# Attention values with the heads' values as 64-column weights and the probabilities moving

## What is computed

```python
# fox_prompt, one block of 128 queries
s = einsum('bqhd,bshd->bhqs', qi, kp) * SCALE + c_q - c_k      # masked to kpos <= qpos
p = softmax(s)
out = einsum('bhqs,bshd->bqhd', p, vp)
# swa: p = exp(s + bias - m) / (sum(exp(s + bias - m)) + exp(sink - m)), out = p @ v
fo = fox(...) * silu(fg); so = swa(...) * silu(sg)
y = layer_norm(ALPHA * x + concat([fo, so]) @ w_out)
```

## Time and profile before

| | us |
|---|---|
| median of 3 runs | 1110.37 |
| lowest, highest | 1108.74, 1110.75 |
| the profiled execution | 1110.16 |
| its span on the core | 1108.6 |
| TensorE busy | 1082.8 (98%) |
| VectorE busy | 556.2 (50%) |
| ScalarE busy | 470.8 (42%) |
| clock granted to TensorE, mean share of full speed | 0.995 |

### The profile page before, as it was taken

How to read it: one execution, slowest core, us unless ns; L and a number is a source line. 1 busy time by engine, 2 the same in 40 slices (tenths; PEclk the granted TensorE clock), 3 DMA queues, 4 the chain that set the end, 5 groups by cost and what they waited for, 6 DMA issues and landing times.

```text
span 1108.6 us, 21056 instructions
## 1 busy us (share of the span) xinstructions
PE 1082.8 (98%) x7697; PEld 1039.1 (94%) x7697; DVE 556.2 (50%) x1330; ACT 470.8 (42%) x1235; POOL 50.4 (5%) x99
## 2 busy tenths in 40 slices
PE   6999999999999999999999999999999999999996
PEld 6999999999999999999999999999999888888885
DVE  6654354444535444444543665453665474424486
ACT  5344444444444444444444555544555553112300
POOL 1010000000000000000000000000000000000000
PEclk9999999999999999999999999999999999999998
DMA  8132223212222222123522122122121216322423
GB/s 336 41 133 88 71 98 105 89 60 106 81 75 98 72 84 87 69 98 105 165 91 96 47 76 83 46 88 86 60 76 52 76 42 243 115 76 76 160 87 114
DMA packets 20376, 106.62 MB, mean 96 GB/s; under 512 B 3168, under 2 KB 3584, under 8 KB 11056
## 3 DMA queue, kind: packets, MB, share of 16 engines
q1 hardware_dynamic: 14528, 83.12, 21.1%
q0 software_dynamic: 5808, 22.95, 6.2%
HBM read 95.18 MB, written 14.17 MB: 99 GB/s over the span
## 4 chain that ended last, share of the span: by engine, by line
PE 97%; DVE 1%; issue 1%; ACT 0%; DMA 0%; DVEq 0%; SPq 0%; ACTq 0%
PE ps L1139 61%; PE ps L1288 19%; PE ps L1248 8%; PE ps L1230 4%; PE ps L1213 2%; PE ps L1214 2%; PE ps L1167 1%; PE ps L1260 1%; PE ps L1272 1%; DMA x_raw<-in_xT 0%; DVE rows L1108 0%; DVE rows L1118 0%; ACT k L640 0%; PE ps L1262 0%; DVE xl L939 0%
## 5 line engine op out<-in xcount | busy, mean ns | idle before, releaser
L1139 PE MATMUL ps<-xh,wh 128*128 128x288 f32 (+1 forms) x1664 | 508.4, 306 | 0.0
L1139 PE MATMUL ps<-xl,wh 128*128 128x288 f32 (+1 forms) x1664 | 492.9, 296 | 0.0
L1139 PE MATMUL ps<-xh,wl 128*128 128x288 f32 (+1 forms) x1664 | 492.4, 296 | 0.0
L1139 PEld LDWEIGHTS ps<-xh,wh 128*128 128x128 f32 x1664 | 313.7, 189 | 0.8 <-DVE wl L944 0.3
L1139 PEld LDWEIGHTS ps<-xl,wh 128*128 128x128 f32 x1664 | 314.1, 189 | 0.0
L1139 PEld LDWEIGHTS ps<-xh,wl 128*128 128x128 f32 x1664 | 313.2, 188 | 0.0
L798 DVE TENSOR_TENSOR wl<-w_raw,wh 128x1024 fp32r<-128x1024 f32 x132 | 159.8, 1218 | 74.5 <-ACT wh L611 72.5
L1288 PE MATMUL ps<-wh,mix_parts 128*128 128x512 f32 x576 | 186.9, 393 | 0.7 <-issue 0.7
L658 ACT ACTIVATE tb<-tb,small 128x256 f32<-128x256 f32 (+5 forms) x160 | 82.4, 515 | 214.1 <-DVE small L886 145.3
L611 ACT ACTIVATE wh<-w_raw 128x1024 fp32r<-128x1024 f32 x132 | 137.9, 1053 | 73.6 <-PE ps L1288 67.5
L1288 PEld LDWEIGHTS ps<-wh,mix_parts 128*128 128x128 f32 x576 | 108.9, 189 | 23.5 <-issue 0.9
(11 more groups left out here) (116 smaller groups left out, 888.3 us busy)
## 6 DMA issues: line engine op xcount, KB each, us to landing
w_raw<-in_w_all SPq DMA_DIRECT2D x66, 1024.0 KB, 4.8
cbc<-c_rows POOLq DMA_DIRECT2D x16, 360.0 KB, 4.2
x_raw<-in_xT SPq DMA_DIRECT2D x8, 592.0 KB, 10.0
rows<-in_x_p POOLq DMA_DIRECT2D x4, 1024.0 KB, 10.6
out_y_p<-rows SPq DMA_DIRECT2D x16, 256.0 KB, 2.5
rel_copies<-rel_rows POOLq DMA_DIRECT2D x1, 3072.0 KB, 16.2
out_fvT<-vT POOLq DMA_DIRECT2D x8, 296.0 KB, 2.4
out_fkT<-kT POOLq DMA_DIRECT2D x8, 296.0 KB, 2.4
```

What stands on the lines that cost most here:

```text
L1139: ins = nc.tensor.matmul(ps[:, st.bank(k, h), 0:width], a[k % 2][:, w], b[:, ko, first:first + width], start=(ko == 0 and i == 0), stop=(k ...
```

## The change

The division moves ahead of the product: after the reciprocal VectorE multiplies the unit's row of probabilities by it, in place (`tensor_scalar`, 160 of them, 144 to 528 columns), and `turn` waits for that (`scaled`) in place of the exponential (`exp_done`). `values` is called once for both heads of a query tile, at the second head's step: for each block and head the 64 columns of `v_nat` are the weights and `pt` moves, 128 columns wide (64 for the sample), and head 0 writes PSUM partitions 0 to 63, head 1 partitions 64 to 127 of the same bank. So the result lies as the gate wants it; `turn_heads`, `normalize` and `o_nat` are gone, and the gate reads the bank of the values. `pt` gets three slots in place of two. In the last stretch a unit is turned three steps after its score instead of two.

```diff
         if final:
-            score, turn, value = [[u + c for u in range(10)] for c in (1, 3, 5)]
+            score, turn, value = [[u + c for u in range(10)] for c in (1, 4, 5)]
...
-                if u >= 2:
-                    act.wait_ge(valued, 10 * st.g + u - 1)
+                if u >= 3:
+                    act.wait_ge(valued, 5 * st.g + (u - 3) // 2 + 1)
...
-            def normalize(st, u):
-
-                index, head = UNITS[u]
-                slot, n = u % 5, 10 * st.g + u + 1
-                act.wait_ge(valued, n)
-                act.wait_ge(recip_done, n)
-                nc.scalar.activation(o_nat[:, index, HD * head:HD * head + HD], ps[:, st.value_bank(u), 0:HD],
-                                     ACT.Copy, scale=recip[:, slot:slot + 1]).then_inc(value_read, 1)
...
                 nc.vector.reciprocal(rc, t).then_inc(recip_done, 1)
...
+                row = tb[:, u % SLOTS, 0:st.kind.keys(QTILE[UNITS[u][0]])]
+                dve.wait_ge(recip_done, n)
+                nc.vector.tensor_scalar(row, row, rc, None, ALU.mult).then_inc(scaled, 1)
...
-                pe.wait_ge(exp_done, 10 * st.g + u + 1)
+                pe.wait_ge(scaled, 10 * st.g + u + 1)
...
+                first, q = (P * tile, P) if tile < 4 else (0, DEC_SEQ)
                 for j, (_, w, block_) in enumerate(blocks):
-                    weights = pt[:, u % 2, j, :] if w == P else pt_meta[:, u % 2, :]
-                    ins = nc.tensor.matmul(ps[:, st.value_bank(u), 0:HD], weights,
-                                           v_nat[:, block_, HD * head:HD * head + HD],
-                                           start=(j == 0), stop=(j == len(blocks) - 1))
+                    for head in range(2):
+                        slot = (2 * index + head) % 3
+                        moving = pt[:, slot, j, 0:q] if w == P else pt_meta[:, slot, :]
+                        ins = nc.tensor.matmul(ps[head_rows(head), st.value_bank(tile), first:first + q],
+                                               v_nat[:, block_, HD * head:HD * head + HD], moving,
+                                               start=(j == 0), stop=(j == len(blocks) - 1))
                 ins.then_inc(valued, 1)
-
-            def turn_heads(st, g):
-
-                pe.wait_ge(value_read, 10 * g + 10)
-                if g is st.turn_before:
-                    pe.wait_ge(v_ready, 4 * st.kvs)
-                for index in (3, 2, 1, 0):
-                    tile = QTILE[index]
-                    ins = nc.tensor.transpose(ps[:, st.heads_bank(0), tile * P:(tile + 1) * P], o_nat[:, index, :], ident[:])
-                ins.then_inc(heads_turned, 1)
-                nc.tensor.transpose(ps[:, st.heads_bank(1), 0:P], o_nat[:, 4, :], ident[:]).then_inc(heads_turned, 1)
```

More of the change, by code:

```diff
@@ L236, in turn_bank, with value_bank_before, value_bank @@
         return 6 if self.final else 4 + p % 2
-    def value_bank(self, u):
-        return 7 if self.final else 6 + u % 2
-    def heads_bank(self, part):
-        return (6 if self.final else 4) + part
+    @staticmethod
+    def value_bank_before(tile):
+        return 6 if tile < 4 else 7
+    def value_bank(self, tile):
+        if self.final:
+            return 7 if tile < 4 else 5
+        return self.value_bank_before(tile)
 def build(nc, xT, w_all, w_ff, b_f, lf_cache, k_cache, v_cache, sinks, rel, keep_k, keep_v,
@@ L587, in _ @@
             whole(pool, run)
-            over = -(-4 * D_MODEL // TOK)
+            over = -(-4 * D_MODEL // NQ)
             for m in range(MT):
@@ L749, in run @@
                         keep_turned(st, u)
-                    for u in st.at(st.value_at, s - 1):
-                        normalize(st, u)
                     if st.kv is not None and s == CACHED_AT:
@@ L1232, in turn, with values @@
                     ins.then_inc(turned, 1)
-            def values(st, u):
-                index, head = UNITS[u]
+            def values(st, index):
                 tile = QTILE[index]
@@ L1239, in values @@
                 pieces = len(st.kind.blocks(tile))
-                if tile == 4 and head == 0:
+                if tile == 4:
                     pe.wait_ge(v_cached, 16 * st.kvs)
-                if u >= st.depth:
-                    pe.wait_ge(value_read, 10 * st.g + u - st.depth + 1)
-                pe.wait_ge(turned_read, st.kind.base(st.g) + st.kind.first(u) + pieces)
-                for j, (_, w, block_) in enumerate(blocks):
-                    weights = pt[:, u % 2, j, :] if w == P else pt_meta[:, u % 2, :]
-                    ins = nc.tensor.matmul(ps[:, st.value_bank(u), 0:HD], weights,
-                                           v_nat[:, block_, HD * head:HD * head + HD],
-                                           start=(j == 0), stop=(j == len(blocks) - 1))
@@ L1251, in values @@
[L1251 to L1262 removed]
+                    if st.final:
+                        pe.wait_ge(score_read, st.kind.base(st.g) + st.kind.PIECES)
@@ new lines, in values @@
+                if index == 0 and st.kind is Swa:
+                    pe.wait_ge(gated, 2 * st.g)
+                pe.wait_ge(turned_read, st.kind.base(st.g) + st.kind.first(2 * index + 1) + pieces)
+                first, q = (P * tile, P) if tile < 4 else (0, DEC_SEQ)
+                for j, (_, w, block_) in enumerate(blocks):
+                    for head in range(2):
[4 more added lines that the diff above has]
+                                               start=(j == 0), stop=(j == len(blocks) - 1))
@@ L1268, in turn_values @@
                 if st.kind:
+                    pe.wait_ge(turned_read, st.kind.base(st.g) + st.kind.PIECES)
                     pe.wait_ge(gated, 2 * st.g + (0 if st.keep else 2))
@@ L1322, in run @@
                     for u in st.at(st.value_at, s):
-                        values(st, u)
+                        if u % 2:
+                            values(st, u // 2)
                     for u in st.at(st.turn_at, s):
@@ L1327, in run @@
                         score(st, u)
-                    if st.turn_before is not None and s == st.before_at:
-                        turn_heads(st, st.turn_before)
-                    if s == st.out_at:
-                        turn_heads(st, st.g)
                     if s == st.v_at:
```

52 lines of the change are left out of this document (24 added, 28 removed).

## The result

The changed kernel takes **1112.73 us** in the median of seven runs (1111.28 to 1114.07), the kernel before beside it 1109.33 (1107.61 to 1110.75). The ratio is 1.0028, 95% interval 1.0019 to 1.0037: slower by 3 us, where 25 us less were forecast. Its profiled execution has a span of 1111.1 us, against 1108.6 before.

What follows compares the result with a forecast made beforehand. TensorE was taken to bound the kernel. Fox stretches -26.5 - 3.8, pair 11 -2.5, tight stretches +8.9 and last stretch -1.45 sum to -25.4 from 1110.16: 1085 us, own range 1076 to 1098, given range 1076 to 1117.

Steps and rivals of the forecast that it cites:

- What bounds the kernel: Whole kernel: TensorE, busy 98% of the span and holding 97% of the chain of waits, bounds it.
- The price of a value instruction: Values on TensorE after the change: between 0.056 and 0.109 us each; the lower taken, with both array halves working together.
- The halves take turns: Rival for the values on TensorE: each instruction costs 0.109 us, whole kernel 1114 us, 1109 to 1121; chance 0.25.
- The ends of a group: Entry and exit of each value group on TensorE: no cost in the sum; 0.1 us per entry would give 1093.
- each change of form empties the array: Rival: every entry and exit of the 80 value groups pays 0.16 us, whole kernel 1107 us, 1098 to 1110; chance 0.09.
- the forecast's slots: Fox pair's values after the change: 32 slots of 0.112 us and 5 of half that, 3.86 us.
- the values before: Fox pair's values on TensorE in the old kernel: 64 instructions, 7.17 us.
- The waits of the tight stretches: Turns wait for VectorE's scaling, a cycle of 2.54 us against TensorE's step of 2.04: 3.64 us a tight stretch.
- the waits don't come: Rival for the tight stretches: VectorE's cycle catches up, whole kernel 1062 us; chance 0.06.
- The heads: Sixteen times five head transposes of 0.109 us leave TensorE, 0.545 us a pair.
- The last stretch: Final stretch: gains 1.6 + 0.55 + 0.5 (the last for `normalize`), less 1.2 us of waits: 1.45 us shorter.

Runs made afterwards that it cites:

- `low_half`: Changed kernel, but value products of both heads go to partitions 0 to 63 and are summed there, so nothing works beside anything: 1152.40 us, ratio 1.0382.
- `after`: The changed kernel itself, with no further edit, measured against the kernel before: 1112.73 us, ratio 1.0028.
- `forms`: Changed kernel, but each query tile's plain float32 value products have another weight shape (64, 48, 32, 64 in the upper half, 16 columns): one execution, 1151.0 us.
- `full_width`: Changed kernel, but every value product has all 128 columns of v_nat as weights and writes all 128 partitions: 1134.02 us, ratio 1.0214.
- `forms_one_pass`: Changed kernel, but outside the last stretch value products are single-pass ones with weights of 64, 48, 32, 128 and 16 columns: one execution, 1081.65 us.
- `heads_apart`: Changed kernel with the value loops exchanged, all blocks of head 0, then all of head 1, in one group: 1123.56 us, ratio 1.0122.

## Why the prediction was wrong

Forecast -25.4 us, measured +2.5 in the profiled spans, 27.9 apart. By its own steps:

**What bounds the kernel** was right: TensorE does. It is busy for 17.5 us less and idle for 20 us more, of which 13.7 + 4.9 are the two waits above.

**The price of a value instruction** was right in the point held most uncertain. The halves work at the same time, a pair takes 0.10 to 0.11 us. *The halves take turns* had 0.25 and a time (1114) that lies next to the measured one, but its mechanism is refuted by the starts 7 ns apart and by `low_half`, 40 us slower. A time that fits proves no mechanism.

**The ends of a group** is the first step that failed. The sum had none; it is the second rival, *each change of form empties the array*, given 0.09. The cost is real. It put 2 x 0.16 us a group, and 0.144 + 0.194 were measured. That the array is quite empty between the two forms is not shown: by the records an instruction still starts 0.07 us before the end of the one before.

In a fox pair five groups pay 5 x 0.34 = 1.7 us. Against this the forecast's slots were 0.6 us too many (32 of 0.112 and 5 of 0.056, where the trace has 28 of 0.109 and 4 of 0.058). That leaves 1.1 of the 1.3 us by which a fox stretch missed. The other 0.2 is the values before, priced at 7.17 us, which took 7.0 from end to end. The eight fox pairs make 10.3 us of the 27.9 (the opening's 0.4 aside). In the tight stretches the ends are a part of the loss: without waits 33.0 was forecast, and 34.45 measured with the turn at five. Of the 1.45 us, 1.0 are the groups' ends less the slots too many, 0.4 is the wait for ScalarE's copies, and 0.1 the price before. With the turn at four the waits were larger than forecast as well, by up to 0.4 us. The six tight stretches miss by 8.4 us in all, pair 11's by 1.2.

The argument against the rival was taken from another kind of instruction, transposes, which pay nothing. The Trainium skill, "TensorEngine Tiling (Array Packing)", Key Properties, had said that a change of tiling mode drains TensorE. The runs fit this for plain float32 products and show 0.34 us; for single-pass products and for transposes among transposes they show none, which that section doesn't tell apart.

**The waits of the tight stretches** were right, and a little too small: 3.64 us forecast, 4.0 added up turn by turn. The turn at five steps took 3.7 off, leaving out the division 3.86. The scaling itself took 354 ns for 256 columns, between the 0.29 taken and the 0.43 held possible. The rival *the waits don't come* is refuted.

**The heads** were right: in the trace of the kernel before, the five transposes take 0.55 us from end to end, in a fox stretch and in a tight one.

**The last stretch** gained 1.0 in place of 1.45. Its first product of the output projection starts 2.77 us after the last of the input projection, where it was 2.94: 0.17 us won, not the 0.5 put down for `normalize`. The products after it run at the lower clock for as long as before, 3.4 us.

**What was left out** is the second failed step: 7.9 us. The diff had it in two lines, `mixT` at 576 columns and `over` counted by them. Neither stood in the sum, since they look like bookkeeping of memory. The loads that they govern had little slack before: VectorE's four sums of the prompt's rows started at 944.2 us, since the sample's rows had kept it waiting (L1069 of the kernel before; durations, first and last start, and what it sat idle for),

```profile
L1069 DVE SCALAR_TENSOR_TENSOR rows<-rows,ps x4: 680/681/689, 944.2 to 946.0; 128x512 f32 x4
...
  DMA rows<-in_x_s: 4.4, 1
```

and TensorE wanted the first bank back at 946.0: 1.1 us. Loads issued 3.3 us later in the stretch (47.7 against 44.4), the last landing 5.0 us later in it, could not hide in that. So a wait whose number changes is a step that moves, and belongs in the sum.

The measured time lies in the given range by luck: the forecast's own was 1076 to 1098, and the wider one reached up to 1117 for the halves by turns, whose mechanism is refuted. 0.74 for faster was too much: the sum asked what each edit costs on its engine, and not which late transfer has slack.

## What to carry to other kernels

Two plain float32 products of 64 weight columns side by side in the array's halves double its pace, but each visit costs a third of a microsecond here: gather many into one group. When work is put ahead of a transpose or product on another engine, work out the cycle between the two engines. Where it is longer than a step (2.5 against 2.04 us), move the transpose a step later too. When a buffer changes size, recount every transfer that waits for parts of what lies over it, and let each wait only for its own part.

## What the runs showed of the hardware

- Plain float32 products with weights of 16 to 64 columns, amid ones of 128: 0.144 us more at entry (64 columns), 0.194 at the exit to a product, 0.15 to a transpose (`after`, `low_half`, `forms`, against `full_width`). Single-pass ones of 32 to 64 columns: none (`forms_one_pass`).
- Instructions of the upper half start beside those of the lower even when they stand behind them in the program, and so before some that stand ahead of them, four deep (`heads_apart`).
- A stream of 128-column plain float32 instructions goes at 109 ns with 64 weight columns and at 112 with 128; with 64 moving columns at 58 and 112.
- In a stop of 4.9 us TensorE's granted clock fell to half; thirteen instructions then ran 0.427 us apart in place of 0.227, and 3.0 us were lost (`after`). At a stop of 2.8 us it fell in some kernels and not in others.
